# Modulation matvec along rows, a gate spread by DMA, and a depthwise convolution moved from GpSimd to VectorE

## The reference, cut to what matters

```
u = cv_a * sigmoid(cv_b)
u = causal_depthwise_conv(u, conv_w, conv_b)      # 31 taps, 512 channels
logf = log_sigmoid(f_logit + b_f);  c = cumsum(logf, axis=positions)   # 8 heads
s = q @ k.T * scale + c[query] - c[key], causal   # fox attention, per head
```

```
mod = silu(c_2) @ w_ada_2 + b_ada_2     # 2048 x 6144 matrix, 48 columns of 128
```

## Time and profile before

| what | value |
|---|---|
| median of three runs | 2100.72 us |
| profiled execution: span | 2099.9 us |
| profiled execution: around the span, taken as the median less the span | 0.8 us |
| TensorE matmul busy | 2005.7 us, 96% |
| VectorE busy | 1125.5 us, 54% |
| ScalarE busy | 772.0 us, 37% |
| GpSimd busy | 605.7 us, 29% |
| mean granted TensorE clock | 0.979 |

### The profile page before, as it was taken

How to read it: one execution, slowest core, us unless ns; L and a number is a source line. 1 busy time by engine, 2 the same in 40 slices (tenths; PEclk the granted TensorE clock), 3 DMA queues, 4 the chain that set the end, 5 groups by cost and what they waited for, 6 DMA issues and landing times.

```text
span 2099.9 us, 26646 instructions
## 1 busy us (share of the span) xinstructions
PE 2005.7 (96%) x9194; PEld 1609.9 (77%) x9194; DVE 1125.5 (54%) x1379; ACT 772.0 (37%) x1054; POOL 605.7 (29%) x446
## 2 busy tenths in 40 slices
PE   5899999999999998999699999999999999998999
PEld 4788777777777775888477777777888887887887
DVE  6723458788875547777633333334445454445332
ACT  4432332322323354222433333334444445544111
POOL 4504888888860000333200000000222222211000
PEclk8999999999999998999899999999999999999999
DMA  6322224444444423676122222222121221212342
GB/s 239 119 100 101 80 103 138 160 160 151 149 144 162 162 92 133 218 237 228 48 83 82 82 82 82 82 82 80 66 75 60 80 80 60 79 60 100 140 140 79
DMA packets 48941, 241.39 MB, mean 115 GB/s; under 512 B 5392, under 2 KB 6544, under 8 KB 28304
## 3 DMA queue, kind: packets, MB, share of 16 engines
q1 hardware_dynamic: 48912, 241.02, 32.7%
HBM read 232.61 MB, written 8.39 MB: 115 GB/s over the span
## 4 chain that ended last, share of the span: by engine, by line
PE 78%; DVE 11%; ACT 4%; issue 4%; DMA 1%; POOL 1%; DVEq 0%; SPq 0%; POOLq 0%; ACTq 0%
PE ps_p L505 23%; PE ps_p L507 22%; PE ps_p L506 22%; DVE ada_acc L1334 5%; DVE w_lo L1146 2%; PE ps_o L583 2%; PE ps_s L563 2%; PE ps_s L730 2%; ACT w_hi L792 1%; PE ps_x L547 1%; DMA mkv<-ada_dram 1%; PE ps_x L629 1%; DVE hd L1554 1%; PE ps_o L764 1%; PE ps_t L573 1%
## 5 line engine op out<-in xcount | busy, mean ns | idle before, releaser
L505 PE MATMUL ps_p<-act_hi,w_hi 128*128 128x512 f32 x2384 | 977.5, 410 | 28.6 <-DVE act_lo L1476 8.7
L507 PE MATMUL ps_p<-act_hi,w_lo 128*128 128x512 f32 x2384 | 938.1, 394 | 0.0
L506 PE MATMUL ps_p<-act_lo,w_hi 128*128 128x512 f32 x2384 | 936.2, 393 | 0.0
L505 PEld LDWEIGHTS ps_p<-act_hi,w_hi 128*128 128x128 f32 x2384 | 452.5, 190 | 144.2 <-issue 44.1
L507 PEld LDWEIGHTS ps_p<-act_hi,w_lo 128*128 128x128 f32 x2384 | 451.9, 190 | 98.0
L506 PEld LDWEIGHTS ps_p<-act_lo,w_hi 128*128 128x128 f32 x2384 | 453.4, 190 | 90.9 <-issue 7.0
L1146 DVE TENSOR_TENSOR w_lo<-raw,w_hi 128x2048 fp32r<-128x2048 f32 x157 | 363.5, 2315 | 230.3 <-ACT w_hi L792 218.4
L792 ACT ACTIVATE w_hi<-raw 128x2048 fp32r<-128x2048 f32 x157 | 300.2, 1912 | 424.0 <-PE ps_p L507 410.0
L1334 DVE SCALAR_TENSOR_TENSOR ada_acc<-mkv,c_act,ada_acc 128x512 f32<-128x512 f32 (+1 forms) x240 | 234.7, 978 | 33.7 <-DMA mkv<-ada_dram 25.9
L1691 POOL TENSOR_TENSOR hkd<-hqk,hd 128x512 f32<-128x512 f32 x8 | 10.4, 1299 | 676.9 <-ACT hd L1095 676.9
L1666 POOL TENSOR_TENSOR Y<-Y,ctmp 128x512 f32<-128x512 f32 x124 | 191.6, 1545 | 9.7
(11 more groups left out here) (226 smaller groups left out, 1687.0 us busy)
## 6 DMA issues: line engine op xcount, KB each, us to landing
raw<-wt_dram SPq DMA_DIRECT2D x157, 1024.0 KB, 4.8
mkv<-ada_dram SPq DMA_DIRECT2D x96, 512.0 KB, 3.3
Y<-xT_dram SPq DMA_DIRECT2D x4, 1024.0 KB, 10.7
qkv<-xT_dram SPq DMA_DIRECT2D x16, 256.0 KB, 2.8
spill_dram<-Y SPq DMA_DIRECT2D x16, 256.0 KB, 2.0
hqk<-spill_dram SPq DMA_DIRECT2D x16, 256.0 KB, 2.7
out_dram<-wk SPq DMA_DIRECT2D x16, 256.0 KB, 2.0
Y<-memT_dram SPq DMA_DIRECT2D x4, 512.0 KB, 7.7
```

The source lines that it names most:

```text
L505: mm(o, wh, hi[:, k, 0:n], start=at == 0, stop=False)
L506: mm(o, wh, lo[:, k, 0:n], start=False, stop=False)
L507: last = mm(o, wl, hi[:, k, 0:n], start=False, stop=at == KT - 1)
```

## The change

The modulation matrix is laid out with output channels on partitions. A piece is now half of the 2048 inputs of 128 output channels, and one `tensor_tensor_reduce` of 128x1024 multiplies it by `c_all`, the activated vector spread over all partitions, and sums along the row. Pieces, their size, their number per head and their places in the lists stay. The two halves are added by VectorE (`ada_out`), with no work on TensorE. `c_all` and the cumulated gates of all eight heads, spread over the partitions into `Y[:, 4:12]`, are made once, by ScalarE's DMAs through DRAM, after "flog"; the spread by matmul, its mask and its copy are gone. The activation of `c_2` moves from the end of memh to the end of flog.

The convolution's 31 taps are now VectorE's, four fused multiply-adds of 128x512 per tap: taps 0 to 2 after the scan in flog, one in each memh head, three in each fox head. GpSimd's loop is gone. The table `starts` gets a buffer and a load of its own ahead of "att".

```diff
+TAPS0, TAPS_MEM, TAPS_FOX = 3, 1, 3
-                project("fox", i, 0, hooks={7: lambda: side("fox", i, 0, spread_c)})
+                project("fox", i, 0)
...
-                                            12: lambda: turn_probs("fox", i, 3, tp[:, 0, :]),
-                                            14: lambda: side("fox", i, 2, ada_sum("fox", i, 1))})
+                                            12: lambda: turn_probs("fox", i, 3, tp[:, 0, :])})
...
-                project("out1", i, 1, order=late, use="y",
-                        hooks={14: lambda: side("out1", i, 0, ada_sum("out1", i, 0))})
+                project("out1", i, 1, order=late, use="y")
```

ScalarE, after the softplus of flog and ahead of memh:

```diff
+            softplus(c_act[:, :], col("c_2", 0, KT)).then_inc(gate_soft.sem, 1)
+            act.wait_ge(gate_log.sem, gate_log.at("flog", 0, 2))
+            fn(c_act[:, :], c_act[:, :], ACT.Exp).then_inc(gate_sig.sem, 1)
+            act.wait_ge(side_in.sem, side_in.at("cums", 0, 1))
+            act.dma_start(cum_rows, cT[0:NFOX, :]).then_inc(s_cum_rows, 16)
+            act.wait_ge(c_ready, 1)
+            act.dma_start(c_row, c_act[:, :]).then_inc(s_c_row, 16)
...
+            act.wait_ge(s_cum_rows, 16)
+            act.dma_start(Y[:, 4:4 + NFOX, :], cum_rows.unsqueeze(0).broadcast_to([P, NFOX, S])).then_inc(s_cum_all, 16)
+            act.wait_ge(s_c_row, 16)
+            act.dma_start(c_all[:, :], c_row.rearrange("p k -> (p k)").unsqueeze(0).broadcast_to([P, D])).then_inc(
+                s_c_all, 16)
```

VectorE:

```diff
+            def conv_tap(tap):
+                w0 = COLS["conv_w"][0]
+                o.settle()
+                for c in range(NCONV):
+                    o.step(stt(Y[:, c, :], upad[:, c, bass.ds(tap, S)], cols[:, bass.ds(tap + (w0 + c * TAPS), 1)],
+                               Y[:, c, :], ALU.mult, ALU.add))
+            for c in range(NCONV):
+                o.step(ts(Y[:, c, :], upad[:, c, 0:S], col("conv_w", c * TAPS), col("conv_b", c), ALU.mult, ALU.add))
+            for tap in range(1, TAPS0):
+                conv_tap(tap)
...
                 split("memh", i, 1)
+                for n in range(TAPS_MEM):
+                    conv_tap(TAPS_MEM * i + (TAPS0 + n))
...
             def ada_step(phase, i, j):
+                    w = ada_ring[:, n % 2, :]
+                    dve.wait_ge(s_ada[n % 2], 8 * per * i + 16 * ((g0 + n) // 2 + 1))
+                    dve.tensor_tensor_reduce(
+                        out=w, in0=w, in1=c_all[:, n % 2 * ADA_PIECE:(n % 2 + 1) * ADA_PIECE], scale=1.0, scalar=0.0,
+                        op0=ALU.mult, op1=ALU.add, accum_out=halves[:, n:n + 1]).then_inc(ada_used, 1)
...
             def fox(i):
-                ts(wk[0:NFOX, 0, :], cT[0:NFOX, :], ident[0:NFOX, bass.ds(i, 1)], None, ALU.mult).then_inc(side_in.sem, 1)
                 split("fox", i, 0)
                 ada_step("fox", i, 0)
+                conv_tap(fox_tap(i, 0))
                 dve.wait_ge(proj_done, tile_no("fox", i, 0) + 2)
                 do(ts(qkv[:, 0, :], ps_p[:, slot("fox", 0), :], SCALE, None, ALU.mult))
                 dve.sem_inc(evac[slot("fox", 0)], 1)
                 split("fox", i, 1)
                 ada_step("fox", i, 1)
+                conv_tap(fox_tap(i, 1))
+                o.settle()
                 dve.wait_ge(proj_done, tile_no("fox", i, 1) + 2)
                 do(dve.tensor_copy(qkv[:, 1, :], ps_p[:, slot("fox", 1), :]))
...
                 ada_step("fox", i, 3)
-                ada_out("fox", i, 3)
+                ada_out("fox", i)
+                conv_tap(fox_tap(i, 2))
```

More of the change, by code:

```diff
@@ L46 @@
 NHG = 8
-ADA = dict(fox=(4, 2), out1=(2, 4))
-ADA_PIECE = 8 * P
+ADA_PIECE = D // 2
+ADA_PER = dict(fox=8, out1=4)
 ADA_AT = dict(fox=(3, 3, 0, 2), out1=(2, 2))
@@ L164, in build @@
         c_act = sb("c_act", [P, KT])
+        halves = sb("halves", [P, 8])
+        whole = sb("whole", [P, 4])
         gall = sb("gall", [P, KT])
@@ L172, in build @@
         wk = sb("wk", [P, 4, S])
-        ones, ident, starts = consts[:, 0:P], consts[:, P:2 * P], consts[:, 2 * P:2 * P + S]
+        ones, ident = consts[:, 0:P], consts[:, P:2 * P]
         eye_b, causal_b, chunk_b = masks[:, 0, :], masks[:, 1, :], masks[:, 2, :]
@@ L219, in build @@
         hS = sb("hS", [P, NCH - 1, P], F32, third)
+        starts = sb("starts", [P, S], F32, third)
         third.close()
@@ L268, in build @@
         heads_done = Count(sem("heads_done"), memh=1, fox=1, att=1, hg=1)
-        gates = dict(conv=1, flog=1, memh=1, cums=1, fox=1, gate=4, att=1, hg=3)
+        gates = dict(conv=1, flog=2, memh=1, fox=1, gate=4, att=1, hg=3)
         gate_soft = Count(sem("gate_soft"), **gates)
@@ L272, in build @@
         gate_sig = Count(sem("gate_sig"), **gates)
[L274 removed]
+        side_full = Count(sem("side_full"), start=1, mem_a=1, xnorm=1, mem_b=1, cums=1, fox=1, gate=2,
                      norm2=1, att=3, hg=3)
[L276 removed]
+        side_free = Count(sem("side_free"), start=1, mem_a=1, xnorm=1, mem_b=1, cums=1, fox=1, gate=2,
                      norm2=1, att=3, hg=3)
[L278 removed]
+        side_in = Count(sem("side_in"), xnorm=2, cums=1, gate=2, att=2, hg=1)
+        c_ready = sem("c_ready")
+        s_c_row = sem("s_c_row")
+        s_c_all = sem("s_c_all")
+        s_cum_rows = sem("s_cum_rows")
+        s_cum_all = sem("s_cum_all")
         ln_ready = Count(sem("ln_ready"), gate=4)
@@ L461, in _ @@
             sp.wait_ge(norm2_tiles.sem, norm2_tiles.at("norm2", 0, 1))
+            sp.dma_start(starts[:, :], starts_d).then_inc(s_starts, 16)
             loop(sp, "att", att)
@@ L644, in fox @@
                                             13: lambda: scores("fox", i, 3, q, k, causal_b)})
-                project("fox", i, 3, hooks={4: lambda: turn_value("fox", i, 1, v, QT),
+                project("fox", i, 3, hooks={4: lambda: turn_value("fox", i, 0, v, QT),
                                             8: lambda: turn_probs("fox", i, 0, tp[:, 0, :]),
@@ L950, in fox @@
                 split("fox", i, 3)
-                value_turned("fox", i, 2, qkv[:, 3, :])
+                value_turned("fox", i, 1, qkv[:, 3, :])
                 for j in range(QT):
@@ L1319, in ada_step @@
             def ada_step(phase, i, j):
-                cols_n, kts = ADA[phase]
-                per, g0, width = KT // kts, ADA_G0[phase], cols_n * P
-                acc = ada_acc[:, 0:width]
+                per, g0 = ADA_PER[phase], ADA_G0[phase]
                 for n in range(sum(ADA_AT[phase][:j]), sum(ADA_AT[phase][:j + 1])):
[L1325 to L1341, removed]
@@ new lines, in ada_out @@
+            def ada_out(phase, i):
+                per, g0, m0 = ADA_PER[phase], ADA_G0[phase], ADA_M0[phase]
+                n = per // 2
+                pair = halves[:, 0:per].rearrange("p (m h) -> p m h", h=2)
+                dve.wait_ge(ada_used, per * i + (g0 + per))
+                do(tt(whole[:, 0:n], pair[:, :, 0], pair[:, :, 1], ALU.add))
+                do(tt(mod[:, bass.ds(n * i + m0, n)], whole[:, 0:n],
+                      cols[:, bass.ds(n * i + (COLS["b_ada_2"][0] + m0), n)], ALU.add))
@@ L1462, in out1 @@
                     dve.sem_inc(residual_tile.sem, 1)
-                ada_out("out1", i, 1)
+                ada_out("out1", i)
             loop(dve, "out1", out1, head=1, order=o)
@@ L1653, in _ @@
                 tt(act_lo[:, k, :], x_ring[k % 3], act_hi[:, k, :].bitcast(F32), ALU.subtract).then_inc(moving, 1)
-            pool.wait_ge(conv_in, 2)
-            for c in range(NCONV):
-                o.step(pool.tensor_copy(Y[:, c, :], col("conv_b", c).broadcast_to([P, S])))
-            o.settle()
-            with pool.Fori(0, TAPS) as tap:
-                o.again()
-                for c in range(NCONV):
-                    w0 = COLS["conv_w"][0] + c * TAPS
-                    o.step(tt(ctmp[:, :], upad[:, c, bass.ds(tap, S)],
-                              cols[:, bass.ds(tap + w0, 1)].broadcast_to([P, S]), ALU.mult))
-                    o.settle()
-                    o.step(tt(Y[:, c, :], Y[:, c, :], ctmp[:, :], ALU.add))
-                    o.settle()
-            pool.sem_inc(conv_out, 1)
             def out1(i):
```

75 lines of the change are left out of this document (28 added, 47 removed).

## The result

The changed kernel takes 2107.85 us (median of 6 runs, 2105.45 to 2109.9) where the kernel before, timed beside it, takes 2101.36: ratio 1.003, 95% interval 1.0019 to 1.0041. The change makes the kernel 0.3% slower, and the forecast of 2106 is 1.9 us off. Its profiled execution spans 2104.7 us (before: 2099.9).

The account below looks back on a forecast made before the run. TensorE was taken as the bound, with 78% of the chain. 2100.7 + 4.5 (fox) + 16.2 (flog, memh) - 13.3 (out1) = 2108 us, lowered to 2106 because two terms lean up; range 2080 to 2132.

Parts of the forecast that it names:

- the copy: VectorE's key copy in each fox head, claimed to end 4.55 us later, at 31.1 or 30.4 us.
- the hook: TensorE's first score matmul in each fox head, claimed to wait 3.65 us for VectorE's key copy; bounds 2.6 and 6.
- The two waits for the third piece: VectorE's 4.24 and 3.49 us idle in a fox head's two steps, claimed to stay, with taps after them.
- base: Fox head without spread and sum over partitions, TensorE never waiting: claimed 50.1 us.
- The clock term: TensorE's loss to low clock behind each fox head's score wait: claimed 1.8 us, between 0 and 2.5.
- Rival A: VectorE's product runs at half rate, 2.3 us, making the fox key copy 2.8 us later: 2128 us; chance 0.18.
- A wait of 6.6: TensorE's wait in us at memh's second tile, whose split stands behind flog's added VectorE work; 8.6 with clock loss.
- The waits of 1.6 us in three heads: TensorE's waits in three memh heads, from the tap between split and maxima; 1 us of low clock added to each.
- 7.0 + 0.9: Out1 gains: 7.0 us from the first round's wait for VectorE and its low clock, 0.9 us per round.
- B: Fox: TensorE hardly loses clock and VectorE's key copy is less late; 2078 us, half way 2090; chance 0.30.
- C: Fox: pieces come early, the key copy isn't late, TensorE bounds the stage at 401; about 2064 us; chance 0.03.

Follow-up runs that it names:

- fox_gap: The changed kernel with both convolution taps of fox steps 0 and 1 moved before the step's last product, into VectorE's wait for the third piece; 2061.0 us.
- mod_only: The changed kernel with the convolution back on GpSimd as before, its temporary in wk, so only modulation, spread and their transfers are changed; 2059.59 us.
- act_order: The changed kernel with only ScalarE's order in flog and memh's head 0 changed: high part before c's exponential and the four DMA issues; 2108.81 us.
- mem_late: The changed kernel with flog's and memh's convolution work moved later, behind memh's first split and the scaling of the probabilities; 2098.45 us.
- fox_half: The changed kernel with only step 1's fox tap moved before the third product, step 0's tap staying behind; 2069.69 us.

## Why the prediction was right, point by point

- **Fox head, wait.** Predicted: the copy ends at 31.1 or 30.4 us of the head, the hook waits 3.65. Measured: 31.1, and 28.1 / 8 = 3.5. The two waits for the third piece stayed, as said, and fox_gap shows that they, and the taps behind them, are all there is.
- **Fox head, base and clock.** 50.1 predicted, 50.1 in fox_gap. The clock term was mis-sized: 447.2 / 8 = 55.9, less 50.1 and 3.5, leaves 2.3 where I had 1.8. The 1.8 holds for five heads (1.8 to 1.95); the other three lost 2.9 to 3.1, since the low level lasted twice as long there, and so the heads are not "all eight alike". This makes the stage 447.2, not 444.6.
- **Tap and product.** 2.73 and 1.22 us; predicted 2.73 and 1.3. Rival A is out: alone, the product runs at full rate. The Trainium skill's rule of half throughput ("Vector Engine (DVE) Microarchitecture Reference", section 7) isn't borne out by this trace: the instruction has two fp32 sources and a sum to read out (0.08 us), and takes 1.22 us for 1024 elements where the plain two-input `split` takes 2.29 for 2048. A product of 2.3 us as A supposed it does come, from GpSimd. Whether it would have cost A's 22 us stays open: in mod_only it made the copy at most 2.1 us later, not 2.8, but there no taps stand behind it and TensorE has no wait; no run has slow products and taps together in fox.
- **Flog.** A wait of 6.6 predicted, 6.28 measured; the first memh head ends 8.0 us later than in the earlier trace rows's kernel (233.05, before 225.07), 0.9 of it inherited from before flog (in the runs here flog's first VectorE row lies anywhere from 198.2 to 200.3, with no pattern that I can name), so that 7.1 are its own; 8.6 predicted. But my sentence that ScalarE's high part, wanted only at 210.7, costs nothing held just because the taps were in front: it was the second cause, and the repair had to deal with it.
- **Memh.** The waits of 1.6 us in three heads came to 1.56, 1.56 and 1.54. The 1 us of clock that I added to each did not come: a head takes 28.0 in place of 26.27. Flog and memh together +13.2, predicted 16.2, bounds 9 to 20.
- **Out1 and after.** Rounds of 21.8 predicted, (886.73 - 864.97) = 21.76 measured. -13.3 predicted, -15.5 measured for all that follows fox. By the read-outs of the second tile of a round, 1.1 us of this is no work of the change: behind a wait of 3.7 us that both kernels have in front of their first tile after fox (796.16 before, 816.46 after), five steps took 6.23 us before and 5.10 after, by the clock. Then come 7.9 us up to the end of the second round, as predicted (7.0 + 0.9), 5.6 in the six others (predicted 5.4), and 0.9 in front of norm2, where TensorE had waited 1.55 us for the bias of the modulation and now waits 0.63 for ScalarE; that wait I had overlooked.
- **Rivals B and C.** B needed wait and clock together under 4.5 us a head; they were 5.8. C's 2064 us was a good number for a kernel that nobody had written yet: 401 us of fox is what TensorE's list allows, and moving the two taps gets there.

The terms add to +7.4 us where the spans differ by 4.8: they were off by -2.6 (fox), +3.0 (flog and memh) and +2.2 (out1 and after), and partly cancel; that the forecast lies 1.9 us off is partly luck. Its last step, 2108 brought down to 2106 because the clock losses were thought too high, was right for memh and wrong for fox. The mechanism, wait by wait, is what the runs bear out.

## What to carry to other kernels

Work that is moved to another engine belongs into that engine's waits: the same two taps in eight heads cost 47 us (2107.85 - 2061.0) behind a wait for a transfer and nothing in front of it. Before pricing a late instruction, ask what is already late beside it: a cause that is covered shows no cost (act_order) until the cover is taken away (mem_late). And when a step is taken out of the bounding engine, look which engine's slowness had reached it through that step; here it was GpSimd's, for the most part through the sums over partitions and the spread (read from the kernel before; not tried one by one).

## What the runs showed of the hardware

- A two-input product of 128x1024 fp32 on VectorE takes 1.22 us alone and 2.05 to 2.32 beside GpSimd's two-input additions, which in turn take 1.26 us at least and 2.27 beside it. It is blocking, not a shared rate: the timelines under mod_only fit one instruction after the other to 0.15 us. Four scalings with a single tensor input were slower as well in three heads of mod_only, 3.0 to 3.1 us for 1.14. In the Trainium skill, "SBUF — State Buffer" says under "Who interferes with whom" that a VectorE instruction with two SBUF inputs contends with a GpSimd instruction that reads SBUF, that the ports they share are an exclusive lock, and that the order of issue decides who blocks; the trace agrees. The prediction had "half the rate" as a property of the instruction only.
- TensorE's clock stayed at 2.4 GHz behind waits of 0.89 to 1.65 us (fox_half) and of 1.56 us (memh), and was at 1.2 GHz behind waits of 2.81 us (mem_late, matmuls of 0.63 in place of 0.39) and of 3.11 to 3.88 (changed kernel). The length of the wait alone doesn't decide: in the fox stage of the kernel before the granted clock fell behind waits of 0.98, 1.38, 1.43, 1.53 and 1.84 us at the spread and the sums over partitions, and stayed at 1.00 behind one of 1.31. Nor does it set how long the low level lasts: of two heads that waited 3.88 us one lost 1.9 us by it and the other 2.9.
